# Weight halves of two neighbouring 128-column tiles stored column by column in turn, and loaded into TensorE with a step of two columns

## The reference

```python
for i in range(DEPTH):                                   # 2 layers
    hn = rmsnorm(x, w['norm_mix_g'][i])
    o = s5_mixer(hn, ...) if i < N_A_LAYERS else nsa_mixer(hn, pos, kv, ...)
    x = x + o
    x = x + swiglu(rmsnorm(x, w['norm_ffn_g'][i]), w['ffn_w_gate'][i],
                   w['ffn_w_up'][i], w['ffn_w_down'][i])  # (silu(h @ wg) * (h @ wu)) @ wd
    gate = jax.nn.sigmoid(rmsnorm(x, w['norm_ple_g'][i]) @ w['ple_w_gate'][i])
    x = x + gate * (p[i] @ w['ple_w_proj'][i])
```

## Time and profile before

| | |
|---|---|
| time, median of 3 runs | 3314.52 us (3307.37 to 3318.40) |
| the profiled execution | 3305.81 us, span of its instructions 3304.0 us |
| granted TensorE clock, mean | 0.992 of full speed |
| PE busy, PEld busy | 98%, 93% of the span |
| DVE, ACT, POOL busy | 62%, 44%, 16% |
| transfers | 608.42 MB, 184 GB/s, DMA engines 40% to 90% busy by slice |

### The profile page before, as it was taken

The page is one execution under the profiler, slowest core; times in us unless marked ns, Lnnn a source line. Parts: engine busy times, 40 slices in busy tenths (PEclk is TensorE's granted clock), DMA queues, the critical chain, the costliest instruction groups (busy, mean ns, idle before and its releaser), DMA issues.

```text
span 3304.0 us, 69206 instructions
## 1 busy us (share of the span) xinstructions
PE 3222.4 (98%) x27708; PEld 3072.9 (93%) x27708; DVE 2034.2 (62%) x2281; ACT 1461.7 (44%) x1927; POOL 539.7 (16%) x477
## 2 busy tenths in 40 slices
PE   7999999999999999999999999998999999999998
PEld 6898889899999999999999997855999999999998
DVE  7999988865655544555665546455655554455566
ACT  4555555643543433343454433344444343334444
POOL 5666566620000000000000006000000000000000
PEclk9999999999999999999999999999999999999999
DMA  6445544455556555655556559888555655665553
GB/s 179 142 146 156 165 151 151 133 168 174 181 178 182 172 189 179 180 172 189 172 178 194 182 185 301 287 283 293 179 182 175 184 179 183 179 178 181 181 171 131
DMA packets 384392, 608.42 MB, mean 184 GB/s; under 512 B 52537, under 2 KB 144986, under 8 KB 383882
## 3 DMA queue, kind: packets, MB, share of 16 engines
q1 hardware_dynamic: 360954, 555.84, 53.9%
q10 hardware_dynamic: 20176, 44.08, 4.0%
q0 software_dynamic: 3024, 5.22, 0.4%
HBM read 594.83 MB, written 26.94 MB: 188 GB/s over the span
## 4 chain that ended last, share of the span: by engine, by line
PE 79%; DVE 13%; POOL 2%; issue 2%; ACT 2%; DMA 1%; SPq 0%; DVEq 0%; POOLq 0%; ACTq 0%
PE psum L399 22%; PE psum L401 22%; PE psum L400 22%; DVE rows_rest L1337 2%; DVE turned L1396 2%; PE psum L2312 2%; POOL prod_pool L1550 2%; PE psum L1016 1%; PE psum L2322 1%; DVE normed_chunk L1421 1%; DVE turned L1387 1%; PE psum L2360 1%; DVE state_ri L1404 1%; PE psum L1037 1%; PE psum L1038 1%
## 5 line engine op out<-in xcount | busy, mean ns | idle before, releaser
L384 DVE TENSOR_TENSOR w_rest<-w_raw,w_head 128x1024 fp32r<-128x1024 f32 x776 | 974.1, 1267 | 958.7 <-ACT w_head L380 957.9
L380 ACT ACTIVATE w_head<-w_raw 128x1024 fp32r<-128x1024 f32 x776 | 812.4, 1057 | 1047.3 <-PE psum L401 1015.9
L399 PE MATMUL psum<-act_head,w_head 128*128 128x264 f32 x4224 | 1206.0, 286 | 5.0 <-DVE act_rest L2743 5.0
L401 PE MATMUL psum<-act_head,w_rest 128*128 128x264 f32 x4224 | 1202.0, 285 | 0.0
L400 PE MATMUL psum<-act_rest,w_head 128*128 128x264 f32 x4224 | 1200.2, 284 | 0.0
L399 PEld LDWEIGHTS psum<-act_head,w_head 128*128 128x128 f32 x4224 | 796.8, 189 | 5.9 <-issue 5.4
L400 PEld LDWEIGHTS psum<-act_rest,w_head 128*128 128x128 f32 x4224 | 798.9, 189 | 0.2
L401 PEld LDWEIGHTS psum<-act_head,w_rest 128*128 128x128 f32 x4224 | 797.4, 189 | 0.0
L399 PE MATMUL psum<-hid_head,w_head 128*128 128x264 f32 x1408 | 401.0, 285 | 0.0
L401 PE MATMUL psum<-hid_head,w_rest 128*128 128x264 f32 x1408 | 400.6, 285 | 0.0
L400 PE MATMUL psum<-hid_rest,w_head 128*128 128x264 f32 x1408 | 399.9, 284 | 0.0
(11 more groups left out here) (421 smaller groups left out, 4075.2 us busy)
## 6 DMA issues: line engine op xcount, KB each, us to landing
w_raw<-in_ffn_w_gate SPq DMA_DIRECT2D x176, 512.0 KB, 3.8
w_raw<-in_ffn_w_up SPq DMA_DIRECT2D x176, 512.0 KB, 4.2
w_raw<-in_ffn_w_down SPq DMA_DIRECT2D x176, 512.0 KB, 3.7
w_raw<-in_cache_cmp_k SPq DMA_DIRECT2D x256, 128.0 KB, 2.6
w_raw<-in_cache_cmp_v SPq DMA_DIRECT2D x256, 128.0 KB, 2.6
w_raw<-in_ssm_w_glu SPq DMA_DIRECT2D x64, 512.0 KB, 4.1
w_raw<-in_ple_w_gate SPq DMA_DIRECT2D x64, 512.0 KB, 4.3
tiles<-in_cache_slc_v SPq DMA_DIRECT2D x128, 256.0 KB
```

The costliest lines, as they stand in the source:

```text
L380: nc.scalar.activation(WH[:, u.slot, :], RAW[:, u.slot, :], ACT.Copy).then_inc(head_done, 1)
L384: nc.vector.tensor_tensor(WL[:, u.slot, :], RAW[:, u.slot, :], WH[:, u.slot, :].bitcast(F32), ALU.subtract).then_inc(rest_done, 1)
L399: nc.tensor.matmul(o, WH[:, u.slot, w], heads[:, k, :], start=k == 0, stop=False)
L401: last = nc.tensor.matmul(o, WL[:, u.slot, w], heads[:, k, :], start=False, stop=k == UK * kunits - 1)
```

## The change

Two neighbouring tiles of 128 columns of a unit (n = 0 and 1, or 2 and 3) are stored in WH and WL in turn: column 0 of the first, column 0 of the second, column 1 of the first, and so on. RAW keeps its order. The copy on ACT still reads RAW in order, and writes each element with a step of two elements (8 bytes); the subtraction on DVE reads RAW in order, reads the head with that step and writes the rest with it. The weight load of a matmul takes its 128 columns with a step of two from WH or WL. The order, number and sizes of all instructions, their waits and the transfers stay as they are.

```diff
--- before.py
+++ after.py
@@ -373,15 +373,21 @@
             sp.wait_ge(rest_done, u.n - (RING - 1))
         sp.dma_start(RAW[:, u.slot, :].rearrange("p (k n) -> p k n", k=src.shape[1]), src).then_inc(raw_ready[u.slot], 16)
 
+    def tiles_of(t, u):
+        return t[:, u.slot, :].rearrange("p (q e c) -> p q e c", e=2, c=P)
+
+    def pairs(t, u):
+        return t[:, u.slot, :].rearrange("p (q c e) -> p q e c", e=2, c=P)
+
     def split_head(act, u):
         act.wait_ge(raw_ready[u.slot], 16 * u.turn)
         if not (u.known and u.n < TAP_UNITS + RING):
             act.wait_ge(units_used, u.n - (RING - 1) - TAP_UNITS)
-        nc.scalar.activation(WH[:, u.slot, :], RAW[:, u.slot, :], ACT.Copy).then_inc(head_done, 1)
+        nc.scalar.activation(pairs(WH, u), tiles_of(RAW, u), ACT.Copy).then_inc(head_done, 1)
 
     def split_rest(dve, u):
         dve.wait_ge(head_done, u.n + 1)
-        nc.vector.tensor_tensor(WL[:, u.slot, :], RAW[:, u.slot, :], WH[:, u.slot, :].bitcast(F32),
+        nc.vector.tensor_tensor(pairs(WL, u), tiles_of(RAW, u), pairs(WH, u).bitcast(F32),
                                 ALU.subtract).then_inc(rest_done, 1)
 
     def group_matmuls(pe, ph, i, c0, kunits, bank, heads, rests, ready):
@@ -393,13 +399,14 @@
                 k = UK * ku + kk
                 if ready is not None:
                     ready(k)
+                head, rest = heads[:, k, :], rests[:, k, :]
                 for n in range(4):
-                    w = slice(kk * UN + n * P, kk * UN + (n + 1) * P)
+                    tile = 2 * kk + n // 2
+                    wh, wl = pairs(WH, u)[:, tile, n % 2, :], pairs(WL, u)[:, tile, n % 2, :]
                     o = PSUM[:, bank + n, 0:T]
-                    nc.tensor.matmul(o, WH[:, u.slot, w], heads[:, k, :], start=k == 0, stop=False)
-                    nc.tensor.matmul(o, WH[:, u.slot, w], rests[:, k, :], start=False, stop=False)
-                    last = nc.tensor.matmul(o, WL[:, u.slot, w], heads[:, k, :], start=False,
-                                            stop=k == UK * kunits - 1)
+                    nc.tensor.matmul(o, wh, head, start=k == 0, stop=False)
+                    nc.tensor.matmul(o, wh, rest, start=False, stop=False)
+                    last = nc.tensor.matmul(o, wl, head, start=False, stop=k == UK * kunits - 1)
             last.then_inc(units_used, 1)
 
 
```

## The result

The changed kernel takes 3329.27 us (median of 6 runs, 3323.19 to 3338.61), the kernel before 3312.80 us (median of 6, 3307.37 to 3318.40): a ratio of 1.0053, with a 95% interval of 1.0035 to 1.0072. It is slower by 16.5 us. The forecast was 3316 us and "within 0.3%" with a chance of 0.68; the measured time lies in the range of 3303 to 3530, but just outside the forecast's own range of 3303 to 3326, on the side that had 0.26.

What follows compares the result with a forecast made beforehand. PE, through its closely following pairs of load and matmul, was taken as the bound. Terms of 0, 0 and 1.5 us on the profiled 3305.81 us gave 3307.3; against the median, 3314.5 + 1.5 = 3316 us; range 3303 to 3530.

Steps and rivals of the forecast that it cites:

- R5: Rival on the split: the forecast's mechanism, but with split durations at their upper ends; up to 3337 us, chance 0.02.
- R2: Rival in PE's pairs: loads and moving operand hinder each other, a stepped load doubles the 9.4 ns; 3491 us, chance 0.08.
- R3: Rival on the split: DVE becomes the bound at 3.18 to 3.34 us per unit; 3526 to 3646 us, chance 0.04.
- The floor of the load: In PE's weight loads: one load of 128 columns can follow another every 112 ns, read from 60-column matmuls.
- Part 1: Term for the projections' weight loads, now with a step of two: 0 us, ends -175 and +756.
- reading (a): Weight load: any stepped read gives one column per some 0.8 ns, the ordinary load's own rate, so nothing is lost: 0 us.
- Reading (b): Weight load: the step adds 0.39 ns per column, 50 ns per load, raising the pair from 121.4 to 162 ns: 756 us.
- R1: Rival on the weight load: the step's surcharge comes on top of the load's time; 4072 us, chance 0.12.
- The load is hidden up to 9.4 ns: In PE's pairs: projection pairs stand 9.4 ns above the load's 112 ns; any slowing by more surely reaches PE.
- Part 2: Split on ACT and DVE: copy at most 1856 ns, subtraction 1267 to 2967 ns, hidden behind PE's 2914 ns per unit.
- Part 3: Where the split is not covered, PE's waits for a rest and the first stage: 1.5 us, ends 0 and 22.
- R4: Rival in PE's pairs: the step takes away part of the 9.4 ns, a gain; 3141 to 3304 us, chance 0.06.

Runs made afterwards that it cites:

- n64_step1: Against the kernel before, weights stored and loaded as there: dense-projection matmuls except each group's first chunk multiply only 64 of 264 token columns; 4923.18 us.
- store_only: Against the changed kernel: heads and rests still written with a step of two, but loads take 128 columns side by side; 3314.27 us, ratio 1.0006 to before.
- n384 kernels: Dense-projection matmuls widened to 384 columns, with the storage and loads of the kernel before (4284.28 us) and of the changed kernel (4307.77 us).

## Why the prediction was right or wrong

**The time.** The forecast had 1.5 us of loss, and 16.5 us were measured. The time lies in the range because the range was drawn upwards over R5 and R2 to the foot of R3, and not because of the forecast's mechanism. It falls where R5 was to lie (up to 3337 us, chance 0.02), but R5's mechanism did not happen: the waits did not grow. That the range holds the time is luck in this sense. Of the signs written down for the forecast, 824 pairs and a load of 189 ns, neither came (818 and 196); a busy share of 98% did.

**What bounds the kernel: right.** PE, with its pairs of load and matmul; the loss is 18,624 times a fraction of a nanosecond, at 18.6 us per nanosecond.

**The floor of the load: right.** 112 ns, read from 60-column matmuls of another stage, are 111.7 in the projections themselves (n64_step1).

**Part 1, the load: the step that failed.** I took reading (a), that an ordinary load is slow enough anyway to lose nothing by a step, at 0 us. The load became 7 ns longer (6 ns at its floor), and 16.6 us came of it, inside the term's ends of -175 and +756. Two things were wrong in it. The transposes of L1853, with all 64 columns in pieces of their own, had shown 0.88 ns per column, and I held this for a limit of any stepped read. An ordinary load with its columns so far apart takes 330 to 339 ns, or (330 - 84) / 128 = 1.9 ns per column: more than double. Reading (b) as I priced it (a pair of 162 ns) was too cheap for such steps as well (232.6 to 241); the clause in R1, "Were it two passes, each slowed so, the price would be higher still", came nearest. That an ordinary load reads each column twice and a transpose once would fit 1.9 against 0.88, but no run separates the passes. And by the count of pieces, which fits the steps of two, three and four, the step of two was mild not because of a common limit but because two of its columns share 16 bytes. My other reason, that 8 bytes are closer to neighbouring columns than 36, was the right one, and it should have been turned into a count of pieces: at 64 pieces the load is where the two limits meet, so a small loss, not none.

**"The load is hidden up to 9.4 ns": half right.** I wrote that a slowing beyond 9.4 ns surely reaches PE, and let everything below count as nothing. Of the 6 ns at the floor, 0.9 came through at 264 columns and 1.26 at 384. A longer load isn't free only because it is still the shorter one, and at 384 columns not even when it is so by 56 ns (174.2 - 117.8).

**Part 2, the split: right.** DVE stayed at 1266 ns; ACT went from 1057 to 1157, within 1057 to 1856; both hidden, as store_only with its 1.0006 shows for itself. ACT's price for a hop, borrowed from DVE, was too low, as the step of four shows. Of the two rules of the Trainium skill that I held against each other, that of "SBUF — State Buffer" fits DVE's 1266 ns, and the estimate of 2.1 to 2.5 us from "Vector Engine (DVE) Microarchitecture Reference" does not fit a step of two; 2051 ns, at a step of four, is close to its 2.1 us. The upper estimate was worked out too low: 2.50 ns times 1024 columns are 2.56 us, just over the cover of 2.54 us, so that "both stay under the cover" did not quite hold for it. The upper end of 2967 ns, made by adding the prices of two hopping streams, does not hold at a step of four: there both hops together cost one price.

**Part 3, the waits: right in kind.** I took 1.5 us; PE's waits for the rest went from 5.7 to 5.6 us. The term should have been nothing.

**The rivals.** R1 did not happen at a step of two, but stands behind the next step: three costs a thousand microseconds. R2 is nearest to what the n384 kernels show, with 0.9 ns in place of 9.4; that the reads of the moving operand are what is hindered is not shown. My doubling rested on the thought that all of the 9.4 ns grow with the width of the read, and they don't. R3, DVE as the bound, did not come up; even the 2051 ns of a step of four, with 370 ns of other work, would stay under the 2914 ns of a unit. R4, a gain, did not either. R5, splits at their upper ends, did not: ACT's 1157 ns and DVE's 1266 are near the lower ones. No version tried is faster than the kernel before, and none of the results points to one.

## What to carry to other kernels

For float32 weights of 128 columns, a step of two elements is nearly free here (0.5% in all through the load, nothing for VectorE, a copy longer by 100 ns and hidden for ScalarE), and a step of three or more is not (load 189, 196, 264, 330 ns for steps of 1 to 4). Count how many pieces of 16 bytes a load touches, rather than how far its elements lie apart; between steps of four and eight, with as many pieces, only 9 ns lie. Where loads and matmuls follow one another without a gap, measure a slower load even if it stays under the matmul's time: here 15% to 21% of the added nanoseconds came through.

## What the runs showed of the hardware that was not expected

- A price read from a transpose's weight load (0.88 ns per column at a step of 36 bytes) does not hold for an ordinary float32 load, which pays about 1.9 ns per column at 16 bytes and 2.0 at 32.
- With 64 moving columns and PE never idle (busy 100.00 of 100 us), the granted clock was 0.50 for most of the time, that is 1.2 GHz in place of 2.4, and a pair took 213 ns in place of 112. It was at 0.50 already from 680 to 720 us, in the first projection, after a mean of 0.98 in the 680 us before. At this clock the stepped load cost nothing (469 and 470 pairs). A narrow matmul behind a full load can thus take longer than one of 264 columns: 213 against 121 ns.
- A pair of load and matmul took 174.2 ns with 384 float32r columns and 121.4 with 264, and a load longer by 6 ns at its floor lengthened both, by 1.26 and 0.89 ns, although that floor (117.8 ns) lies below either.
- A hop in both an input and the output of DVE's subtraction cost 0.77 ns per element, no more than a hop in one of them had in other instructions; ACT's copy paid 0.99 per element for its output alone.
